# Two expert passes of a mixture layer run as one pass of 84 weight units

## The reference, cut to what matters

```python
logits = h @ router_w + router_b
top_val, top_idx = lax.top_k(logits, 2)
combine = sum(one_hot(top_idx, 8) * softmax(top_val)[..., None], axis=-2)
for e in range(8):
    gate, up = split(h @ w_gu[e], 2)          # w_gu[e]: 1024 x 3584
    out += combine[..., e:e+1] * ((silu(gate) * up) @ w_down[e])   # 1792 x 1024
```

## Time and profile before

| | us |
|---|---|
| median of the runs | 1427.14 (1422.32 to 1427.29) |
| the profiled execution | 1430.14 |
| its span | 1428.5 |
| PE busy | 1340.5 (94%), 6707 matmuls |
| DVE busy | 906.7 (63%) |
| ACT busy | 707.6 (50%) |
| POOL busy | 207.7 (15%) |
| moved by DMA | 337.75 MB, mean 236 GB/s |

### The profile page before, as it was taken

One profiled execution on the slowest core, in us unless ns is written; L12 is line 12 of the kernel. 1 busy time (PEld: TensorE's weight loads), 2 busy tenths in 40 slices (PEclk: granted clock), 3 DMA queues, 4 the chain that ended last, 5 costly groups with the idle time before them and its releaser, 6 DMA issues.

```text
span 1428.5 us, 19720 instructions
## 1 busy us (share of the span) xinstructions
PE 1340.5 (94%) x6707; PEld 1082.0 (76%) x6707; DVE 906.7 (63%) x1210; ACT 707.6 (50%) x1121; POOL 207.7 (15%) x277
## 2 busy tenths in 40 slices
PE   6999889999999989999989899998999999999985
PEld 2766468999999968878877687886578778788752
DVE  0425557363333378467776797767999898655676
ACT  1323565232322342433434685556778787544563
POOL 1010000071000005333210534103200000000020
PEclk9999999999999999999999999999999999999998
DMA  9786664458444413666754899866999999976691
GB/s 340 239 298 233 212 222 124 136 186 293 129 133 133 124 42 101 177 209 204 234 198 140 287 383 364 272 219 205 365 370 366 370 368 371 367 219 191 206 363 64
DMA packets 253477, 337.75 MB, mean 236 GB/s; under 512 B 16142, under 2 KB 209964, under 8 KB 253260
## 3 DMA queue, kind: packets, MB, share of 16 engines
q1 hardware_dynamic: 241354, 299.57, 63.7%
q0 software_dynamic: 11792, 37.03, 7.6%
q10 hardware_dynamic: 242, 0.01, 0.0%
HBM read 317.62 MB, written 17.88 MB: 235 GB/s over the span
## 4 chain that ended last, share of the span: by engine, by line
PE 71%; DVE 9%; DMA 8%; ACT 4%; SPq 3%; issue 3%; POOL 0%; DVEq 0%; ACTq 0%
PE PS L2512 18%; PE PS L534 12%; PE PS L2520 9%; PE PS L509 7%; PE PS L511 7%; PE PS L510 7%; PE PS L675 3%; SPq L2156 2%; DMA BIG<-in_moe_w_down 2%; DMA raw<-in_moe_w_gu 2%; DVE wlo L2193 2%; ACT whi L2187 1%; DMA BIG<-in_poolm 1%; PE PS L1511 1%; PE PS L700 1%
## 5 line engine op out<-in xcount | busy, mean ns | idle before, releaser
L485 DVE TENSOR_TENSOR wlo<-raw,whi 128x1024 fp32r<-128x1024 f32 x130 | 164.4, 1288 | 223.9 <-ACT whi L482 223.6
L2193 DVE TENSOR_TENSOR wlo<-BIG,whi 128x1024 fp32r<-128x1024 f32 x180 | 223.8, 1255 | 63.9 <-ACT whi L2187 62.3
L2187 ACT ACTIVATE whi<-BIG 128x1024 fp32r<-128x1024 f32 x180 | 189.6, 1058 | 65.5 <-PE PS L2512 31.8
L2512 PE MATMUL PS<-whi,Hh 128*128 128x512 f32 x540 | 221.3, 410 | 0.4 <-DVE Hl L2343 0.4
L509 PE MATMUL PS<-Hh,whi 128*128 128x384 f32 (+1 forms) x624 | 210.6, 337 | 2.6 <-DVE wlo L485 1.4
L2512 PE MATMUL PS<-wlo,Hh 128*128 128x512 f32 x540 | 212.7, 394 | 0.0
L511 PE MATMUL PS<-Hh,wlo 128*128 128x384 f32 (+1 forms) x624 | 207.1, 332 | 0.0
L510 PE MATMUL PS<-Hl,whi 128*128 128x384 f32 (+1 forms) x624 | 207.0, 332 | 0.0
L2193 DVE TENSOR_TENSOR wlo<-raw,whi 128x1024 fp32r<-128x1024 f32 x138 | 167.7, 1226 | 53.9 <-ACT whi L2187 52.9
L2187 ACT ACTIVATE whi<-raw 128x1024 fp32r<-128x1024 f32 x138 | 145.2, 1059 | 60.4 <-PE PS L2520 28.0
L482 ACT ACTIVATE whi<-raw 128x1024 fp32r<-128x1024 f32 x130 | 133.4, 1051 | 82.3 <-DMA raw<-in_w_in_a 63.0
(11 more groups left out here) (412 smaller groups left out, 2071.1 us busy)
## 6 DMA issues: line engine op xcount, KB each, us to landing
raw<-in_moe_w_gu SPq DMA_DIRECT2D x224, 256.0 KB, 7.0
BIG<-in_moe_w_gu SPq DMA_DIRECT2D x224, 256.0 KB, 6.7
raw<-in_ada_w SPq DMA_DIRECT2D x96, 512.0 KB, 6.3
BIG<-in_moe_w_down SPq DMA_DIRECT2D x80, 512.0 KB, 8.0
raw<-in_ffn_w_gu SPq DMA_DIRECT2D x44, 512.0 KB, 4.7
raw<-in_w_in_c SPq DMA_DIRECT2D x32, 512.0 KB, 6.3
raw<-in_moe_w_down SPq DMA_DIRECT2D x32, 512.0 KB, 8.1
raw<-in_ffn_w_down SPq DMA_DIRECT2D x22, 512.0 KB, 3.7
```

What stands on the lines that cost most here:

```text
L485: self.eng.tensor_tensor(wlo[:, s, :], raw[:, s, :], whi[:, s, :].bitcast(f32), ALU.subtract).then_inc(lo_made, 1)
L2187: act.activation(whi[:, slot(v), :], moe_raw(v), ACT.Copy).then_inc(hi_made, 1)
L2193: dve.tensor_tensor(wlo[:, slot(v), :], moe_raw(v), whi[:, slot(v), :].bitcast(f32), ALU.subtract).then_inc(lo_made, 1)
L2512: last = pe.matmul(PS[:, 6 * b + c % 2, :], lhs, wt[:, 512 * k:512 * k + 512], start=(q == 0 and k == 0 and i == 0), stop=(q == 3 and k == ...
```

## The change

The twin and the few expert run as one pass of 84 units, `PAIR_ORDER`. A is the twin expert (a full and a half block), B the few expert (a half block). Their chunks alternate: A's four gate/up units, B's four, B's two down units of the chunk before, A's two down units of this chunk. Within A's gate/up, units 2 and 3 first do their full block, then their half block. One PSUM bank (0) holds A's full block and then B's, bank 1 A's half block and then the transposes, banks 2 and 3 A's full result, 4 and 5 A's half result, 6 and 7 B's. The two half blocks' tokens lie side by side in the table (`ROW_TWIN` + 128 to `ROW_TWIN` + 255) and are fetched, transposed and cut together ("both"); their results are gathered in one tile (`pair_y`: A's in rows 0 to 63, B's in 64 to 127) and stored at once. Raw units are gone from the last pass too: all units are split, and SP waits only for low parts.

```diff
-ROW_LAST, ROW_FEW, ROW_FIRST, ROW_TWIN, ROW_BIG, ROW_ONE = 0, 64, 128, 256, 448, 704
+ROW_LAST, ROW_FIRST, ROW_TWIN, ROW_FEW, ROW_BIG, ROW_ONE = 0, 64, 192, 384, 448, 704
-NATIVE = tuple(range(8, 42, 4))
+        PAIR_ORDER = []
+        for c in range(MC):
+            PAIR_ORDER += [("A", "gu", c, q) for q in range(4)] + [("B", "gu", c, q) for q in range(4)]
+            if c:
+                PAIR_ORDER += [("B", "dn", c - 1, q) for q in range(2)]
+            PAIR_ORDER += [("A", "dn", c, q) for q in range(2)]
+        PAIR_ORDER += [("B", "dn", MC - 1, q) for q in range(2)]
...
             def one_pass(x, e):
                 for v in range(UB):
-                    if x.whole(v - MRING):
-                        sp.wait_ge(unit_used, x.p * UB + (U_MOE + v - MRING + 1))
-                    else:
-                        sp.wait_ge(lo_made, x.splits(v - MRING))
+                    sp.wait_ge(lo_made, x.splits(v - MRING))
...
-            one_pass(twin_pass(), by_count(1))
-            one_pass(few_pass(), by_count(5))
+            pair(pair_pass(), {"A": by_count(1), "B": by_count(5)})
...
+        def act_pair(act, x):
+            for w, (side, kind, c, q) in enumerate(PAIR_ORDER):
+                act.wait_ge(unit_used, x.used(w))
+                if (side, kind, q) == ("A", "gu", 2):
+                    act.activation(gp[:, 0, c % 2, :], PS[:, 0, 0:256], ACT.Silu).then_inc(esilu_made[0], 1)
+                if (side, kind, q) == ("A", "gu", 3):
+                    act.activation(half_gu, PS[0:64, 1, :], ACT.Copy).then_inc(esilu_made[1], 1)
+                if (side, kind, q) == ("B", "gu", 3):
+                    act.wait_ge(etr_made[0], MC + c + 1)
+                    act.wait_ge(etr_made[1], 2 * c + 1)
+                    act.activation(gu_cols(gu_h, Hh, 0, c), turned_first(), ACT.Copy).then_inc(eguh_made[0], 1)
+                    act.activation(pair_gu("A")[:, :, 0:64], pair_turned("A"), ACT.Copy).then_inc(eguh_made[1], 1)
+                    act.activation(half_gu, PS[0:64, 0, :], ACT.Copy).then_inc(esilu_made[1], 1)
+                if (side, kind, q) == ("A", "dn", 0):
+                    act.wait_ge(etr_made[1], 2 * c + 2)
+                    act.activation(pair_gu("B")[:, :, 0:64], pair_turned("B"), ACT.Copy).then_inc(eguh_made[1], 1)
+                act_unit_hi(act, w + RING, x)
+                if (kind, q) == ("gu", 3):
+                    act.wait_ge(eprod_made[1], 4 * c + (1 if side == "A" else 3))
+                    act.activation(half_gu[:, 0:256], half_gu[:, 0:256], ACT.Silu).then_inc(esilu_made[1], 1)
+                if (side, kind, c, q) == ("A", "dn", MC - 1, 1):
+                    act_tokens(act, 0, 2, False, (1, 0))
...             # y of A's full block, then y of A's half block
+        def dve_pair(dve, x):
+            for w, (side, kind, c, q) in enumerate(PAIR_ORDER):
...             # A gu 2: full product. A gu 3: wait esilu_made[1], add the rows of A's half
+                if (side, kind, q) == ("B", "gu", 3):
...                 # low part of A's full product, low part of A's half product
+                    dve.wait_ge(esilu_made[1], 4 * c + 3)
+                    dve.tensor_tensor(half_gu, half_gu, PS[64:128, 0, :], ALU.add).then_inc(eprod_made[1], 1)
...             # A dn 0: low part of B's product
+                dve_unit_lo(dve, w + RING, x)
+                if (kind, q) == ("gu", 3):
+                    dve.wait_ge(esilu_made[1], 4 * c + (2 if side == "A" else 4))
+                    dve.tensor_tensor(half_gu[:, 0:256], half_gu[:, 0:256], half_gu[:, 256:512], ALU.mult
+                                      ).then_inc(eprod_made[1], 1)
...
+        def pe_pair(pe, x):
...
+            for c in range(MC):
+                if c:
+                    pe.wait_ge(egul_made[1], 2 * c)
...             # A gu 0, 1: full and half block each; A gu 2, 3: full, full, then half, half
+                w += 4
+                pe.wait_ge(eprod_made[0], MC + c + 1)
+                for q in range(4):
+                    pe.wait_ge(lo_made, x.splits(w + q))
+                    unit_gu(w + q, q, 0, 256, False).then_inc(unit_used, 1)
+                w += 4
+                pe.wait_ge(eprod_made[1], 4 * c + 2)
...             # four transposes: A's full product, A's half product
+                if c:
+                    down_b(w, c - 1)
+                    w += 2
+                pe.wait_ge(egul_made[0], MC + c + 1)
+                pe.wait_ge(egul_made[1], 2 * c + 1)
...
+                for q in range(2):
+                    pe.wait_ge(lo_made, x.splits(w + q))
+                    unit_dn(w + q, c, q, 2, gu_cols(gu_h, Hh, 0, c)[:, q, :], gu_cols(gu_l, Hl, 0, c)[:, q, :])
+                    unit_dn(w + q, c, q, 4, pair_gu("A")[:, q, :], None).then_inc(unit_used, 1)
+                    if q == 0:
+                        pe.wait_ge(eprod_made[1], 4 * c + 4)
...                     # two transposes: B's product; in the last chunk also four of tokens
+                w += 2
+            pe.wait_ge(egul_made[1], 2 * MC)
+            tokens(4, 0).then_inc(tok_turned[0], 1)
+            down_b(w, MC - 1)
+            pe.wait_ge(y_made[1], 1)
+            pe_tokens(pe, 1, 1, (4, 5))
...
             fetch(0, 2, ROW_ONE)
-            fetch(1, 1, ROW_FEW)
-            store(0, 2, ROW_TWIN + 64, 128)
-            store(1, 1, ROW_TWIN, 64)
...
+            fetch(1, 1, ROW_BIG + 128)
+            pool_pick(pool, ch)
+            store(0, 2, ROW_TWIN, 128)
+            store(1, 2, ROW_TWIN + 128, 128)
```

More of the change, by code:

```diff
@@ L2120, in sp_experts, with load @@
         def sp_experts(sp):
-            def load(e, v):
-                kind, c, q = E_ORDER[v]
+            def load(e, v, what):
+                kind, c, q = what
                 dst = moe_raw(v)
@@ L2146, in sp_experts @@
                     sp.wait_ge(hn_turned, 6)
-                for dst, src in load(0, v):
+                for dst, src in load(0, v, E_ORDER[v]):
                     sp.dma_start(dst, src).then_inc(moe_full[v % MRING], 16)
@@ L2168, in sp_experts, with landed, full_value @@
             one_pass(last_pass(ns), NE - 1)
[L2170 to L2178, removed]
+        def landed(order, v):
+            return sum(32 if order[x][-3] == "gu" else 16 for x in range(v + 1) if x % MRING == v % MRING)
+        def full_value(v, x):
+            r, end = v % MRING, UB - MRING
+            before = 16 * sum(1 for n in range(U_MOE) if n % RING == (U_MOE + r) % RING) if r < RING else 0
+            one, two = landed(E_ORDER, end + r), landed(PAIR_ORDER, UB + end + r)
+            if x.first:
+                return before + (landed(E_ORDER, v) if v < UB else one + landed(PAIR_ORDER, v - UB))
+            if x.pair:
+                return before + one + (landed(PAIR_ORDER, v) if v < 2 * UB else two + landed(E_ORDER, v - 2 * UB))
+            return x.p * one + (before + two - 2 * one + (landed(E_ORDER, v) if v < UB else one + landed(E_ORDER, v - UB)))
         def act_unit_hi(act, v, x):
-            if x.whole(v):
-                return
-            first, per = full_value(v)
             if v < RING:
                 act.wait_ge(unit_used, U_MOE - RING + v + 1)
-            act.wait_ge(moe_full[v % MRING], x.p * per + first)
+            act.wait_ge(moe_full[v % MRING], full_value(v, x))
             act.activation(whi[:, slot(v), :], moe_raw(v), ACT.Copy).then_inc(hi_made, 1)
         def dve_unit_lo(dve, v, x):
-            if x.whole(v):
-                return
             dve.wait_ge(hi_made, x.splits(v))
@@ L2230, in __init__, with used @@
                 self.first = isinstance(p, int) and p == 0
+                self.single = q1 is None and not self.first
                 self.stored0 = stored0
-            def whole(self, v):
-                return v % UB in self.units[1 + v // UB]
             def splits(self, v):
-                before, here, after = (len([x for x in u if x + at <= v]) for u, at in zip(self.units, (-UB, 0, UB)))
-                return self.p * UB + (S_MOE + v + 1 - self.lost - before + len(self.units[0]) - here - after)
+                return self.p * UB + (S_MOE + v + 1)
+            def used(self, v):
+                return self.p * UB + (U_MOE + v + 1)
             def silu1(self, n):
@@ L2646, in pool_experts @@
             stored(0, m + 3)
[L2647 removed]
+            fetch(1, 2, ROW_LAST)
             store(0, m + 4, ROW_BIG, 128)
```

181 lines of the change are left out of this document (133 added, 48 removed).

## The result

| | median of runs, us | ratio to the kernel before (95%) |
|---|---|---|
| before | 1427.08 (12 runs) | |
| changed | 1432.01 (1427.68 to 1436.19, 12 runs) | 1.004 (1.0026 to 1.0055) |

The change costs 4.9 us, inside what the prediction called the same (7.1 us), but with an interval clear of 1: a small loss and not none. The profiled execution took 1436.19 us, its span is 1434.4, 5.9 more than before. Of these 1.94 lie ahead of anything the change touches: the first expert pass starts at 808.11 and not at 806.17 (in the traces further down it starts anywhere from 800.95 to 808.11, so this is scatter). The rest is found from the starts of the passes.

The account below looks back on a forecast made before the run. TensorE alone bounds the twin pass, neither TensorE nor DMA the few pass, and weights arrive barely in time in single passes. Pair pass +5.7, single passes -3.0, last pass -1.0: +1.7 us, median 1429, range 1417 to 1441.

Parts of the forecast that it names:

- A settled chunk: Pair pass, one repeating chunk: 22.2 us, from 9.1 PE, 0.7 hand-over, 7.3 DVE, 5.0 PE; six take 133.2.
- the walk: Instant-by-instant reading of one settled pair-pass chunk from its first matmul: PE waits 1.5 us before A's down units.
- rival 1: Pair pass: TensorE bound, DVE's late step comes in time, a chunk takes 20.3, total 1417.5; chance 0.12.
- rival 2: Pair pass: clock falls at the wait before A's down units in every chunk, +12, 1441; chance 0.14.
- Chunk 0: Pair pass's first chunk: 22.2, plus 9 for DVE waiting on GpSimd's norm, plus 2.4 for low clock, 33.6 us.
- half of them: Chunk 0: half of A's down-unit matmuls (4.6 us) run at half clock, adding 2.4 us.
- Ends: Pair pass's ends: 0.5 us ahead for token copies; behind chunk 6, 7.0 plus 1.7 for clock, together 8.7.
- Single passes: Three single passes after the pair pass: DMA's lead lets each take 61.2, 183.7 against 186.7, -3.0 us.
- Last pass: Last pass without its nine raw units: DVE nearly full, DMA's hole closes, -1.0 us, bounds -4 and +6.
- Rival 3: Last pass becomes DVE-bound: +6 us instead of -1, 1436; chance 0.12.
- rival 4: Chunk 0 hardly meets GpSimd: 33.6 becomes 25 to 27 us, total 1421; chance 0.10.
- PE's sum: Pair pass: a chunk's 84 matmuls and six transposes on PE, 20.3 us, the bound if the order hid everything.

Follow-up runs that it names:

- tuned kernel: Changed kernel with normalisation beside the big pass, A's products cut one unit earlier, B's product transposed behind A's second down unit: 1416.30 us, 0.9948.
- one reordering: Changed kernel with ACT's and DVE's cutting of A's products moved one unit earlier, before B's third gate/up unit: 1433.17 us, 1.0052.

## Why the prediction was right, and where not

The forecast was no measurable change, 1429 us for a median, in a range of 1417 to 1441; 1432.01 was measured. By its own steps, in the trace (the 1.94 us of before the change left out): +4.0 measured, +1.7 predicted.
- **A settled chunk: 22.2, measured 22.53.** The mechanism held: one wait before A's down units, behind DVE's saturated stretch, and every instant of the walk within 0.2 us. The miss is 0.2 us up to where PE goes on and 0.2 behind it. Five at 22.53 (chunk 6, which has no start behind it, taken as the others) and chunk 1 at 22.79 make 135.4 for 133.2, +2.2, the largest miss. Rivals 1 and 2 did not come: no fall of the clock in chunks 1 to 6.
- **Chunk 0: 33.6, measured 32.35.** That the norm is the cause is shown by moving it (24.1). Its make-up differed: waits of 5.45 and 3.0, not 4 and 8. Three DVE operations were held up (3.06, 2.67 and 2.56 us), then three low halves ran through, 3.48 for the three, while one GpSimd operation took 5.83; after A's low parts two more were held up, a low half (2.02) and B's multiply (2.58). Against a settled chunk PE goes on 5.4 us later at the first down unit, and 2.8 later again at the second, which waits for that multiply: 8.2 for my 9. The second unit at half clock adds 1.7, for my 2.4. My "half of them" was wrong, both units ran at half clock, but over the first it was hidden.
- **Ends.** 0.5 for the token copies, measured 0.7 (the pass's start 2.67 later less the 1.94). The tail 7.0, measured 7.4; its wait 2.8, measured 2.9; the clock's share 1.7, measured 1.8, in the first single pass (10.02 for 36 matmuls). This last agreement is in part luck, since the same wait left the clock up in other runs of this order (8.45).
- **Single passes: -3.0.** 183.7 predicted, measured 185.5 less that 1.8 = 183.7. The size was right and the reason was not: I gave it to DMA's lead behind the pair pass, and the old order without raw units has it too. That is luck.
- **Last pass: -1.0, measured -0.4.** DVE nearly full, the last low half done at 1405.9, which is 174.3 behind the big pass's start (before 173.9). Of the 10.2 us of extra DVE work almost none showed because DMA's waits had left it idle. Rival 3 did not come, rival 4 neither.
- **PE's sum, 20.3 a chunk, was 0.8 too low** (21.1 to 21.2 in the changed and the tuned kernel), and with it rival 1's time. The walk had two of the hand-overs, 0.2 us each, as waits of PE, so its 22.2 suffers less. A slip in the chances: half of rival 3's 0.12 is 0.06, which makes slower 0.27 and the same 0.51.
- **The weakest step** is one in the chunk's reading. The walk listed B's multiply "19.1, before PE wants it at 19.5" and the low part of B's product "21.7, before 22.15" as cover. It did not say that 0.4 us of slack behind each makes them bounds: DVE is saturated for 12 us a chunk, not for 7.3. That didn't harm the forecast of this kernel, but made me expect 6 to 8 us from one reordering that gave none.

Why is the kernel as changed slower? Two things are shown, each by a run that takes back most or all of the loss: GpSimd's norm in chunk 0 (moved: 0.9989 for 1.0040) and the order of DVE's results (tuned: 1.0009). They don't reduce to a price of joining as such. With the norm in place the joined pass takes 2.9 us more than two passes without raw units (175.2 against 172.3); with the norm late it takes 2.1 less (166.5 against 168.6). PE's wait of 1.4 us in each chunk is not the price either, since removing it alone gained nothing. With order and norm both mended the pass takes 158.2 us against 163.2 for the best old order that was run. In the whole time the two lie close, 0.9948 and 0.9969, with intervals that overlap, and how much the old order would gain from a tuning of its own is open.

## What to carry to other kernels

Averaging the load of two phases need not gain anything while an engine that works in its written order delivers its results late: walk one period with the written order of each engine, and list for every result its slack, not only the one that is late first. Two small edits, each worth nothing alone, gave the gain together. Before moving work, look whether two engines that hold each other up in the trace meet at the busiest moment: moving six GpSimd operations gave 7 us, more than the whole change moved. And a low clock costs only where nothing later holds the engine anyway: look at what it waits for next.

## What the runs showed of the hardware

DVE and GpSimd do not alternate strictly: three 1.2 us operations of DVE went through back to back (3.48 us) while one of GpSimd's waited, 5.83 us instead of 2.4. And the clock of PE can fall after waits shorter than the 2.74 us of the earlier trace rows: without B's matmuls PE waited at most 1.8 us before A's transposes and 1.4 before its down units, and in three of six chunks (1, 4 and 6) the granted clock fell. Stretches of that kernel, columns as before:
```profile
912.50:915.90 3.40, 2.87 (x8) 1.81 (x7) 3.34 (x5) 2.29 (x5) 3.30 (x3) 0.53 0.84 258
981.00:984.00 3.00, 2.65 (x7) 1.59 (x6) 2.94 (x6) 1.81 (x5) 0.00 (x0) 0.50 0.73 236
1024.00:1028.00 4.00, 3.42 (x10) 2.63 (x11) 3.98 (x5) 4.00 (x7) 0.00 (x0) 0.62 0.77 239
```
A longer wait does not always bring it down: behind 2.9 us at the pair pass's end the clock stayed at 1.00 in this kernel and in the changed one with the late norm:
```profile
1037.14 8.45 PE PS L2588 x36
```
That is how near rival 2 was: with 1.8 us more waiting in each chunk it began to come, at a price of 0.3 us in chunk 4 (22.84) and 0.1 in chunk 1 (22.92 for 22.79), since DVE hid the rest.
